# DVE chains between units, inverse roots on DVE, silu gates at read-out, and a query norm folded into the exponential, in a four-layer transformer kernel

## The reference

```
first kind:  h = rms_norm(x); p = h @ w_in            # 6560 columns
  mla  : two normed latents -> q, k, v; rope; causal softmax attention, 8 heads
  moba : causal softmax attention, 8 heads of 64
  ret  : retention, 4 heads; o = (o - mean) * rsqrt(var + eps) * gn_w + gn_b; o = silu(g) * o
  x += (sigmoid(g1)*(mla@w) + sigmoid(g2)*(moba@w) + sigmoid(g3)*(ret@w)) @ w_out
  x += square(relu(rms_norm(x) @ w_up)) @ w_down
second kind: u = rms_norm(h); split(u @ w_in)
  gla  : la = log_sigmoid(ra @ w_alpha + b_alpha)/16, both directions; chunked linear attention
         o = rms_norm(o_f + o_b) * g_gla_out, per head of 256; o * silu(gg) @ w_o_gla
  gqa  : q, k = axial_rope(rms_norm(.) * g), 8 query and 2 key heads of 128; softmax(q k / sqrt(128)) v
  h += rms_norm((sigmoid(ga)*gla + sigmoid(gb)*gqa) @ w_out); then a gated feed-forward and an embedding gate
```

## Time and profile before

| | us |
|---|---|
| three timed runs | 2107.15, 2104.64, 2107.12 (median 2107.12) |
| the profiled execution | 2107.21 |
| span of its trace | 2105.2 |
| mean granted TensorE clock | 0.960 of full |
| PE busy | 1955.0 |
| DVE busy, ACT busy | 1234.9, 989.0 |

### The profile page before, as it was taken

How to read it: one execution, slowest core, us unless ns; L and a number is a source line. 1 busy time by engine, 2 the same in 40 slices (tenths; PEclk the granted TensorE clock), 3 DMA queues, 4 the chain that set the end, 5 groups by cost and what they waited for, 6 DMA issues and landing times.

```text
span 2105.2 us, 24832 instructions
## 1 busy us (share of the span) xinstructions
PE 1955.0 (93%) x9157; PEld 1594.2 (76%) x9157; DVE 1234.9 (59%) x1940; ACT 989.0 (47%) x1483; POOL 166.0 (8%) x68
## 2 busy tenths in 40 slices
PE   7999899999988899999897899999798979999996
PEld 6777688888877788887675687888676757878885
DVE  6754653547644663555578456665556784666655
ACT  5446454444436354444434545454444245464544
POOL 0000048200000058100000000000000000000000
PEclk9999999999999899998999999999889999999998
DMA  6534455556433555654433334646543333446562
GB/s 220 143 108 120 151 181 177 184 183 185 137 100 111 160 182 178 187 179 143 130 116 100 120 130 159 190 143 219 155 123 120 115 100 131 140 150 199 156 206 80
DMA packets 167891, 316.49 MB, mean 150 GB/s; under 512 B 12238, under 2 KB 20380, under 8 KB 167644
## 3 DMA queue, kind: packets, MB, share of 16 engines
q1 hardware_dynamic: 167184, 313.17, 47.8%
q10 hardware_dynamic: 588, 1.73, 0.2%
HBM read 313.81 MB, written 1.05 MB: 150 GB/s over the span
## 4 chain that ended last, share of the span: by engine, by line
PE 86%; DVE 7%; ACT 4%; issue 2%; DMA 0%; ACTq 0%; DVEq 0%
PE acc L537 74%; PE mix L509 4%; PE mix L565 2%; DVE lo L1261 1%; PE mix L546 1%; PE mix L772 1%; ACT hi L934 1%; PE mix L696 1%; PE mix L725 1%; PE mix L738 1%; PE mix L734 1%; PE mix L762 1%; ACT junk L978 1%; DVE x L1333 1%; DVE proj L1617 0%
## 5 line engine op out<-in xcount | busy, mean ns | idle before, releaser
L934 ACT ACTIVATE hi<-raw 128x1024 fp32r<-128x1024 f32 x600 | 633.9, 1060 | 707.0 <-PE acc L537 674.7
L1261 DVE TENSOR_TENSOR lo<-raw,hi 128x1024 fp32r<-128x1024 f32 x536 | 646.4, 1226 | 255.1 <-ACT hi L934 240.8
L537 PE MATMUL acc<-hi,xTh 128*128 128x512 f32 (+3 forms) x1760 | 707.2, 402 | 76.8 <-DVE lo L1261 69.0
L537 PE MATMUL acc<-lo,xTh 128*128 128x512 f32 (+3 forms) x1760 | 690.5, 392 | 0.0
L537 PE MATMUL acc<-hi,xTl 128*128 128x512 f32 (+3 forms) x1760 | 690.3, 392 | 0.0
L537 PEld LDWEIGHTS acc<-hi,xTh 128*128 128x128 f32 x1760 | 343.4, 195 | 156.3 <-issue 90.0
L537 PEld LDWEIGHTS acc<-hi,xTl 128*128 128x128 f32 x1760 | 342.2, 194 | 69.1
L537 PEld LDWEIGHTS acc<-lo,xTh 128*128 128x128 f32 x1760 | 343.4, 195 | 62.6
L913 POOL TENSOR_TENSOR lo<-raw,hi 128x1024 fp32r<-128x1024 f32 x64 | 165.8, 2615 | 684.8 <-ACT hi L934 684.5
L537 PE MATMUL acc<-hi,hTh 128*128 128x512 f32 x432 | 171.8, 398 | 0.0
L537 PE MATMUL acc<-hi,hTl 128*128 128x512 f32 x432 | 171.2, 396 | 0.0
(11 more groups left out here) (199 smaller groups left out, 1665.2 us busy)
## 6 DMA issues: line engine op xcount, KB each, us to landing
raw<-in_w_in SPq DMA_DIRECT2D x200, 512.0 KB, 3.8
raw<-in_w_ffn_in SPq DMA_DIRECT2D x80, 512.0 KB, 4.2
raw<-in_w_mlp_up SPq DMA_DIRECT2D x64, 512.0 KB, 3.8
raw<-in_w_mlp_down SPq DMA_DIRECT2D x64, 512.0 KB, 4.5
raw<-in_w_ffn_out SPq DMA_DIRECT2D x44, 512.0 KB, 4.3
raw<-in_w_out SPq DMA_DIRECT2D x32, 512.0 KB, 4.4
raw<-in_w_o_gla SPq DMA_DIRECT2D x16, 512.0 KB, 3.8
raw<-in_w_o_attn SPq DMA_DIRECT2D x16, 512.0 KB, 3.6
```

The source lines that it names most:

```text
L537: last = nc.tensor.matmul(out, a[:, t * P:(t + 1) * P], w[:, slot, part, 0:c.n], start=(k == 0 and a is ah and w is L.hi), stop=(k == c.k_ ...
L934: nc.scalar.activation(L.hi[:, slot], L.raw[:, slot], ACT.Copy).then_inc(*n.up("hi_ready"))
L1261: v.tensor_tensor(L.lo[:, slot], L.raw[:, slot], L.hi[:, slot].bitcast(F32), ALU.subtract).then_inc(*n.up("low_by_dve"))
```

## The change

- `inverse_root`, a bit-shift first guess and three Newton steps, eleven linked DVE instructions on narrow columns, takes the place of ACT's Sqrt and `refine` in all norms but the three `add_normed` of each second layer.
- Retention: the root goes to step 1, and steps 2 (normalise), 3 (gain and bias) and 4 (gate) stand beside MOBA heads 2, 3 and 4.
- The silu gates (RG; GG) become chunks named "silu": ACT writes the sigmoid when the accumulators are read out, DVE multiplies into it in place of its scaled copy.
- The opening of layer 2 is spread over units 2, 3, 4 and 5.
- The bias of alpha becomes a 17th row of the product; ACT makes |z|, and DVE's part is put between units 16 to 20.
- GLA output squares are accumulated by ACT from PSUM; its gain is folded into the split (`gain_col`); norm and gate are one instruction for each head and tile (`gla_out`), beside GQA heads 0 and 1.
- Query norm: its inverse root goes into the exponential's scale (`Q_SCALE`) and the shift; gains are folded into rope tables (`make_turns`, unit 10); all heads are roped by unit 44; q and k are turned at unit 46, and the GQA heads start at unit 48 with two units for each; the GLA halves are turned beside heads 2 and 5.

```diff
+    def inverse_root(var, out, width):
+        r, va, a = col(out, width), col(var, width), col(NEWTON, width)
+        link(v.tensor_scalar(a.bitcast(I32), va.bitcast(I32), 1, None, ALU.logical_shift_right))
+        link(v.tensor_scalar(r.bitcast(I32), a.bitcast(I32), -1, 0x5F3759DF, ALU.mult, ALU.add))
+        for _ in range(3):
+            link(v.tensor_tensor(a, r, r, ALU.mult))
+            link(v.scalar_tensor_tensor(out=a, in0=a, scalar=-0.5, in1=va, op0=ALU.mult, op1=ALU.mult))
+            link(v.scalar_tensor_tensor(out=r, in0=a, scalar=1.5, in1=r, op0=ALU.add, op1=ALU.mult))
...
+        elif c.name == "silu":                     # ACT, in after(c); then DVE, in read_out(c)
+            act.wait_ge(*n.at("unit_used", c.final + 1))
+            for t in range(NT):
+                last = nc.scalar.activation(L.proj[:, t, c.to:c.to + COLS], pair(c)[:, t], ACT.Sigmoid, scale=L.small[:, PRE + t:PRE + t + 1])
+            last.then_inc(*n.up("glu_ready"))
...
-        softmax_heads("moba", MOBA_H, MOBA_D ** -0.5, 0, MOBA_UNITS, lambda h: retention_out(h) if h < 2 else None)
+        softmax_heads("moba", MOBA_H, MOBA_D ** -0.5, 0, MOBA_UNITS, lambda h: retention_out(h) if h < 5 else None)
         s.to(50)
         split_half("moba", 0)
-        retention_out(2)
...
+        s.to(3)                                    # opening_after_final
+        mean_of_parts()
+        inverse_root(VAR_X, FINAL, NT)
+        s.to(4)
         dve.wait_ge(*n.next("squared", 2 * NT))
...
+        inverse_root(VAR_X, PRE, NT)
         link(v.tensor_tensor(col(PRE, NT), col(PRE, NT), col(FINAL, NT), ALU.mult))
+        s.to(5)
...
         for d in range(2):                         # ACT, unit 16
-            act.wait_ge(*n.next("minus_abs"))
-            nc.scalar.activation(L.soft[:, d], L.soft[:, d], ACT.Exp).then_inc(*n.up("logarithm"))
+            for t in range(NT):
+                b = filled(("gla", "z", d, t))
+                nc.scalar.activation(L.soft[:, d, t, :], L.mix[:, b, :], ACT.Abs).then_inc(*n.up("magnitude"))
+            act.wait_ge(*n.next("magnitude", NT))
+            nc.scalar.activation(L.soft[:, d], L.soft[:, d], ACT.Exp, scale=-1.0).then_inc(*n.up("logarithm"))
             s.on(1)
...
             gla_states(h)                          # DVE, units 30 to 42
             if h == 1:
-                query_norms(0, 4)
+                head_squares(0, 4)
             elif h == 2:
-                query_rope(0, 4)
+                for t in range(NT):
+                    head_rope(0, 4, t)
+            elif h == 3:
+                head_squares(4, 8)
+                for t in range(NT):
+                    head_rope(4, 8, t)
             s.on(3)
+        head_squares(8, 10)
+        s.on(1)
+        head_roots()
+        for t in range(NT):
+            head_rope(8, 10, t)
...
+        s.to(44)
+        dve.wait_ge(*n.next("squared", NT * GLA_H))
+        link(v.tensor_scalar(col(VAR_G, 8), col(VAR_G, 8), NORM_EPS, None, ALU.add))
+        inverse_root(VAR_G, ROOT_G, 8)
...
+        s.to(46)
         empty(("gqa", "k", 0), L.kT[:, 0:2, :], 2 * TOK)
+        s.to(48)
         for h in range(AQ_H + 2):
...
+            if h < 2:
+                gla_out(h)
+            if h == 2:
+                split_half("gla", 0, gla_gain(ln))
+            if h == 5:
+                split_half("gla", 1, gla_gain(ln))
             if h == 8:
                 split_half("attn", 0)
-            s.on(1 if 1 <= h <= 8 else 0)
+            s.on(2 if 1 <= h <= 8 else 0)
```

More of the change, by code:

```diff
@@ L1483, in retention_out @@
             link(last)
+        elif step == 3:
             for i, op in enumerate((ALU.mult, ALU.add)):
@@ new lines, in make_turns @@
+    def make_turns():
+        for kind in range(2):
+            g = L.params[:, kind * A_D:(kind + 1) * A_D].rearrange("p (a s d) -> p a s d", a=2, s=2)
+            c, sn = (L.cst(f"{w}_ax", NT, 64).rearrange("p t (a d) -> p t a d", a=2) for w in "cs")
+            first, second = (spread(g[:, :, i, :], 1, NT) for i in range(2))
+            for out, table, gain in zip(turns(kind), (c, sn, c, sn), (first, first, second, second)):
+                last = v.tensor_tensor(out, table, gain, ALU.mult)
+        link(last)
@@ new lines, in head_squares, with head_roots @@
+    def head_squares(first, end):
+        rows = [(h, t, proj[:, t, at2(AQ) + h * A_D:at2(AQ) + (h + 1) * A_D]) for h in range(first, end) for t in range(NT)]
+        for i, (h, t, r) in enumerate(rows):
+            last = mean_square(L.tmp[:, i % 8 * A_D:(i % 8 + 1) * A_D], r, col(VAR + 2 * h + t))
+        link(last)
+    def head_roots():
+        inverse_root(VAR, ROOT, 2 * (AQ_H + AKV_H))
+        link(v.tensor_scalar(col(Q_SCALE, 2 * AQ_H), col(ROOT, 2 * AQ_H), A_D ** -0.5, None, ALU.mult))
+        for h in range(AQ_H, AQ_H + AKV_H):
+            for t in range(NT):
+                r = proj[:, t, at2(AQ) + h * A_D:at2(AQ) + (h + 1) * A_D]
+                last = v.tensor_scalar(r, r, col(ROOT + 2 * h + t), None, ALU.mult)
+        link(last)
@@ new lines, in head_rope, with gla_out @@
+    def head_rope(first, end, t):
+        r = proj[:, t, at2(AQ) + first * A_D:at2(AQ) + end * A_D].rearrange("p (h a s d) -> p h a s d", a=2, s=2, d=A_D // 4)
+        c, sn, c_b, s_b = (spread(a[:, t], 1, end - first) for a in turns(first // AQ_H))
+        rope(r[:, :, :, 0, :], r[:, :, :, 1, :], c, sn, [end - first, 2, A_D // 4], L.tmp, c_b=c_b, s_b=s_b)
+    def gla_out(g):
+        for h in (2 * g, 2 * g + 1):
+            for t in range(NT):
+                r = y[:, t, h * GLA_V:(h + 1) * GLA_V]
+                gate = proj[:, t, at2(GG) + h * GLA_V:at2(GG) + (h + 1) * GLA_V]
+                last = v.scalar_tensor_tensor(out=r, in0=r, scalar=col(ROOT_G + 2 * h + t), in1=gate, op0=ALU.mult, op1=ALU.mult)
+        link(last)
+        tell("rows_ready")
@@ L1665, in second_layer @@
                 b = filled(key)
-                drain(v.tensor_tensor(la[:, t], mix[:, b, :], bias, ALU.add), key)
-            link(v.scalar_tensor_tensor(out=L.soft[:, d], in0=la, scalar=-1.0, in1=la, op0=ALU.mult, op1=ALU.min), "minus_abs")
-        for d in range(2):
-            la = y[:, :, d * COLS:(d + 1) * COLS]
-            link(v.tensor_scalar(la, la, 0.0, None, ALU.min))
+                dve.wait_ge(*n.next("magnitude"))
+                drain(v.tensor_scalar(la[:, t], mix[:, b, :], 0.0, None, ALU.min), key)
+            s.on(1)
+        s.on(1)
         for d in range(2):
```

260 lines of the change are left out of this document (111 added, 149 removed).

## The result

Timed against the kernel before on one chip, the changed kernel took 2049.49 us in the median (2049.07 to 2050.76) against 2107.09 (2104.64 to 2107.15): a ratio of 0.973, interval 0.9714 to 0.9747. The forecast was 2027 with a range of 2006 to 2052, so the time is in the range, and 22 us above the forecast itself. It is not in 2006 to 2043, where the forecast was to hold on its own. The profiled execution took 2049.88 us, 57.3 less than the 2107.21 of before; the mean granted clock rose from 0.960 to 0.974 of full speed.

A forecast was written before the change was run, and what follows sets the result against it. PE's matmul stream and what interrupts it were taken as the bound. Savings A to E (23.8 + 5.6 + 15.3 + 27.8 + 7.6 = 80.1 us) from 2107.2 gave 2027 us, range 2006 to 2052.

The forecast's parts named there:

- A: Retention tail, layers 0 and 1: PE's waits before unit 52 and the clock loss go; saves 23.8 us.
- rival 2: Layers 0 and 1: wait at unit 52 passes to ACT's work at unit 50, 5 us; 2037 us, chance 0.10.
- B: Opening of layer 2: chain cut at units 3, 4 and 5, still 1.9 us late; saves 5.6 us.
- C: Softplus, layers 2 and 3: DVE serves low parts between pieces, so wait and clock loss go; saves 15.3 us.
- D: Units 39 to 48, layers 2 and 3: saves 27.8 us, 1.0 and 3.1 us waits left at units 41, 45.
- E: GQA heads, layers 2 and 3: two units per head hide PE's waits for turned probabilities and k; saves 7.6 us.
- The sign that I had named as wrong: GQA heads: ACT named as the releaser of PE's waits would show the forecast wrong.
- The other roots: Roots before units 8 and 77 to 83: no PE wait behind them, so counted as 0.
- Rival 4: Some 31 DVE pieces between units each cost a low part and a clock fall; slower, 2119 us, chance 0.04.
- Rival 1: Units 39 to 48, layers 2 and 3: DVE's backlog takes back the whole gain; 2055 us, chance 0.14.
- Rival 3: GQA heads: table switches hold ACT 1.4 us beyond the load, PE waits 2.8 us; 2038 us, chance 0.04.

## Why the prediction came out as it did

- *The range* held by luck. 2049.5 lies in the part from 2043 to 2052 that was added for rivals 1 to 3, and none of these came true.
- *A*: right, -24.4 by the traces and -25.4 alone, forecast -23.8. The waits before unit 52 are gone and nothing took their place, so rival 2 fell; the silu read-out costs 0.54 us at unit 32 (taken: 0.6).
- *B*: right, -5.4 of -5.6.
- *C*: right in its mechanism, and low by 2. Of the 2, 1.5 is unit 16 of layer 2, at the lower clock before and not after, and at the lower clock again in most later runs: scatter, not the chain. In layer 3 the stretch gave 7.7, as forecast. ACT's absolute values took 0.53 to 0.60 us each, not 0.64, and loaded no table: between the two exponentials of this stretch (ACT's timeline, layer 2) the row left out is a high part, and none is a load:

```profile
993.65 1.06 ACT L1134 ACTIVATE soft<-soft 128x1024 f32<-128x1024 f32 x1
...
995.57 1.07 ACT L1132 ACTIVATE soft<-mix 128x512 f32<-128x512 f32 x2
996.66 1.06 ACT L1134 ACTIVATE soft<-soft 128x1024 f32<-128x1024 f32 x1
```

- *D*: right, -26.1 of -27.8. The two waits were forecast to a third of a microsecond (1.0 and 3.1, found 1.20 and 2.81). The clock behind them cost 2.9 us in layer 2 and 1.5 in layer 3, where I had 2.0: unit 45 and the twenty transposes behind it took 7.71 and 6.32 us, against 4.82 in the run with the late rotation, which has no wait there. The granted clock from 1118.72 to 1123.98 is 0.50. No wait in units 39 to 48 is over 3 us. My working put one root and the rotation ahead of that low part, and the runs bear it out: taking the second root away brought nothing, moving the rotation 8.4 us.
- *E*: -4.0 of -7.6, and wrong in its mechanism. Two units for each head were to hide both waits. The wait for k is gone (2.0 us over both layers; the other 2.0 of the 4.0 were not taken apart), the wait for the copy of the turned probabilities is not: 7.1 us in the list of waits above, where the kernel before had this:

```profile
PE mix L772 <- ACT attnT L948: 6.9, 6, 2.1
```

The table loads that I counted as "just fits" did not fit: the head with a gate's sigmoid made PE wait 3.1 us in layer 2 and 2.4 in layer 3, and the run with tanh, which takes these loads away, took 2.5 us out of unit 49 in each layer. The sign that I had named as wrong, ACT as the releaser in the GQA heads, is there; but it was there before too, so it could not tell the two apart.
- *The step that failed* is the sentence "The other roots (before units 8 and 77 to 83) had no PE wait behind them: 0." It looked for waits that would go, and took a root on DVE alone as eleven instructions of the same price everywhere. Beside POOL's low parts five of them cost 2.3 us, the chain stands ahead of halves that PE needs at unit 80, and the new wait with its clock is +15.1 us (14.4, 13.8 and 14.2 when it is taken away in three ways). That is two thirds of the 22.8 us between the sum of 80.1 and the 57.3 found. D, E and B together are 5.5 of the rest, less 2.7 that A and C gave over; 4.9 are small and scattered, in part a clock that fell at other units, and were not tested.
- Rival 4 had the shape of it, a piece that makes PE wait and then costs the clock, but everywhere and cheap; it was one place and dear. Rival 1 (backlog takes D) is refuted by D's 26.1. Rival 3 fell too: after a table load of 1.28 us the next activation began at once, as in the rows above (1142.77 and 1144.07). The 2.66 us for a switch that the Trainium skill gives (ScalarE: Activation LUTs, "What ACT_TABLE_LOAD costs") did not show.

## What to carry to other kernels

When a chain of tiny vector instructions is put somewhere, look at what GpSimd runs there: each one can wait for a whole GpSimd instruction, and a chain waits many times. Put such a chain behind what PE needs next, not ahead of it; the same instructions one unit later were worth 14.4 and 8.4 us here. And count an edit that removes no wait as a possible new one, by the work that it puts ahead of the next thing PE needs.

## Not expected of the hardware

A DVE instruction on 128x2 elements took 0.16 us alone and 2.25 to 2.33 beside POOL, ending with POOL's instruction. DVE's instructions that read PSUM kept their time: four of 128x256 took 1.65 us in the run whose POOL was idle there, and 1.66 in the run with the root behind the halves, where POOL was busy until 290.34 (timelines of DVE and POOL):

```profile
289.07 1.66 DVE L1294 SCALAR_TENSOR_TENSOR xTl<-mix,gain_cols,xTh 128x256 fp32r<-128x256 f32 x4 [5.34 <-ACT xTh L966]
```

```profile
283.22 7.12 POOL L917 TENSOR_TENSOR lo<-raw,hi 128x1024 fp32r<-128x1024 f32 x3 [3.60 <-ACT hi L944]
```

After a wait of 2.8 us the clock took 2.9 us from unit 45 and the turns behind it in layer 2 of the changed kernel, 1.5 in layer 3, and 0.1 in both layers of the run with the softplus chain as before: the same wait has not the same price twice. Tanh and the exponential alternated without a load in between (32 loads in that run, 44 in its base).
